# The layout of the split activations in SBUF for 14,928 products of 288 columns: one run of 288 or four blocks of 72

## The chip, the cores and the metric

The kernel runs on one core of a Trainium2 chip. The metric is the time of one execution on the device, in microseconds (us). All inputs, weights and outputs are float32.

## What is computed

One layer of a streaming encoder for 288 tokens (256 of a prompt, 32 of a sample), which share all weights:

```
x = x + 0.5 * (silu(h @ w_gate) * (h @ w_up)) @ w_down      h = rmsnorm(x)      D = 2048, D_FF = 5504
z = rmsnorm(x) @ w_in                                       37 strips of 128 columns
x = x + concat(A, B, C) @ w_out                             A sparse, B windowed, C banded attention
x = x + 0.5 * (silu(h @ w_gate) * (h @ w_up)) @ w_down      second set of weights
```

Keys and values of the three attentions are outputs too. Nearly all arithmetic is in the eight weight matrices; the attention works on 288 tokens only.

## The kernel before, in words

**Products.** Activations lie with the features on the partitions and the 288 tokens along the free dimension. A weight matrix comes from HBM in strips of 128 output features: a strip is up to 16 tiles of 128 by 128 (15 or 14 in the down projections, whose 43 input tiles are taken in thirds). To get more precision out of the one-pass type float32r, each operand is split in an upper and a lower part: `w_hi` is the weight rounded to float32r (ScalarE, line 1056), `w_lo` the rest (VectorE, line 1367), and likewise `h_hi`/`h_lo` for the normalized input, `gu_hi`/`gu_lo` for the gated product, `o_hi`/`o_lo` for the attention's output. For each tile of a strip TensorE makes three products into the same PSUM bank (lines 601 to 603, in `products`): w_hi times hi, w_lo times hi, w_hi times lo. Each has its own weight load. There are 3 x (3344 + 1376 + 256) = 14,928 of them.

**The right sides.** `right_side` (line 144) gives each of the six activation arrays tiles of TILE = 320 float32 columns, of which columns 24 (PAD) to 311 hold the 288 tokens. `products` reads them backwards, `t[:, ::-1]`, and writes the bank backwards too (lines 598 and 600), so the result stands in its normal order.

**Who writes the right sides.** `h_hi` ScalarE line 1066 and `h_lo` VectorE lines 1376 and 1616; `gu_hi` ScalarE line 1273 and `gu_lo` VectorE line 1692; `o_hi` ScalarE line 1136 and `o_lo` VectorE line 1489. Tile 5 of `o_hi` and of `o_lo` (`key_hi`, `key_lo`) serves for a time as room for squares, which POOL writes and TensorE reads forwards at lines 660 and 661. The first two tiles of `gu_hi` serve as data for ten warm-up products (line 912).

**Order.** Each engine runs its own program; semaphores join them. TensorE goes through the strips of a phase (up, down, prep, cb, a, wo) in a loop; before the first tile of each half strip it waits for that half's `w_lo` (`lo_rdy`), before a strip for the bank two strips back to be read (`evac`). ScalarE and VectorE split the following strip while TensorE multiplies this one; SP's queue loads the strip after that. The weight buffers are double. In a "down" phase TensorE waits at tile 0 for all but the last gated tile and at the last tile for the last one (`gu_when`, line 967); in the first strip after a "down" or "wo" phase it waits before each tile k for `h_lo` of that tile (`h_when`, line 941).

**Other products.** The mean of squares for a norm is one product of 288 columns in plain float32 (line 648), which the profile shows as two passes, each with a weight load. The attention's scores, transposes and outputs are smaller products between the strips of cb and a.

Of the kernel before, what the change touches and what calls it, by code (L numbers as in the profile page):

```python
# [7 lines left out]
ALU = mybir.AluOpType  # L8
ACT = mybir.ActivationFunctionType
AX_X = mybir.AxisListType.X  # L10
F32 = mybir.dt.float32


F32R = mybir.dt.float32r

P = 128
# [97 lines left out]
def encoder_step(nc, x, cak, cav, caki, cbk, cbv, cck, ccv, w_in, w_out, qk_norm, sinks, c_bias, t5_bias,  # L114
# [6 lines left out]
    NT = T_P + T_S  # L121
# [9 lines left out]
    ctx = ExitStack()  # L131
    with ctx:
        def sb(name, shape, dt=F32, scope=ctx):
            return scope.enter_context(nc.sbuf_tensor(name, shape, dt))
# [7 lines left out]
        xT = x_room[:, 3 * DT:3 * DT + DT * NT].rearrange("p (k n) -> p k n", n=NT)  # L142
        def right_side(name, tiles, scope=ctx):
            room = sb(name, [P, tiles, TILE], F32R, scope)
            return room[:, :, PAD:PAD + NT], room

        TILE = -(-NT // 64) * 64
        PAD = 24
        h_hi, _ = right_side("h_hi", DT)
        h_lo, _ = right_side("h_lo", DT)  # L150
        raw = [sb(f"raw{s}", [P, 16, P]) for s in range(2)]
# [6 lines left out]
        with ExitStack() as ffn_scope:  # L158
            gu_hi, gu_room = right_side("gu_hi", thirds[0], ffn_scope)
            gu_lo, _ = right_side("gu_lo", thirds[0], ffn_scope)  # L160
        o_hi, _ = right_side("o_hi", 16)
        o_lo, _ = right_side("o_lo", 16)

# [9 lines left out]
        table_first = sb("table_first", [P, 3])  # L173
        warm = gu_room[:, 0:2, :].rearrange("p k n -> p (k n)")[:, 0:512]

# [30 lines left out]
        sq_set = [t[:, 0:NT] for t in sq_wide]  # L206
        key_hi, key_lo = o_hi[:, 5, :], o_lo[:, 5, :]
        sqx = sq
# [383 lines left out]
        def _(pe):  # L592
            def products(ph, j, s, rhs, ks, n, first_k, last_k, when=None, bank=None):

                for k in ks:
                    if when:
                        when(k)
                    hi, lo = (t[:, ::-1] for t in rhs(k))
                    b = buf(ph, s)
                    out = (bank or bank_w[b])[:, 0:NT][:, ::-1]  # L600
                    pe.matmul(out, w_hi[b][:, k, :], hi, start=(k == first_k), stop=False)  # L601
                    pe.matmul(out, w_lo[b][:, k, :], hi, start=False, stop=False)  # L602
                    mm = pe.matmul(out, w_hi[b][:, k, :], lo, start=False, stop=(k == last_k))  # L603
                return mm
# [24 lines left out]
            def h_rhs(k):  # L629
                return h_hi[:, k, :], h_lo[:, k, :]  # L630

            def gu_rhs(k):
                return gu_hi[:, k, :], gu_lo[:, k, :]

            def o_rhs(k):
                return o_hi[:, k, :], o_lo[:, k, :]

# [385 lines left out]
        def _(act):  # L1023
# [41 lines left out]
            def h_upper(index, j):  # L1065
                act.activation(h_hi[:, j, :], xT[:, j, :], ACT.Copy, scale=g_cols[:, bass.ds(j + index * DT, 1)]).then_inc(hhi_rdy, 1)

# [66 lines left out]
            def out_hi(U, p, tile):  # L1134
                act.wait_ge(pv_done, U + (3 * p + 3))
                act.activation(o_hi[:, tile, :], bank_o[:, 0:NT], ACT.Copy).then_inc(ohi_rdy, 1)

# [106 lines left out]
            for ph in phases:  # L1244
                if ph.name == "up":
                    F0 = sum(p.more["size"] for p in phases[:phases.index(ph)] if p.name == "up")

                    def body(j, ph=ph, F0=F0):
# [23 lines left out]
                        act.wait_ge(gu_rdy, F + 1)  # L1272
                        act.activation(gu_hi[:, j, :], gu[:, :], ACT.Copy).then_inc(guh_rdy, 1)  # L1273
                    bodies(act, ph, body, peel_first=3 if ph.n0 == 0 else ph.more["first"])
# [68 lines left out]
        def _(dve):  # L1343
# [26 lines left out]
            def h_tile(index, j):  # L1370
                H = j + DT * index
                dve.wait_ge(sqx_rdy, H + (1 - DT))
                dve.wait_ge(acc_rdy, H)
                dve.tensor_tensor(sumsq[:, :], sumsq[:, :], sqx[:, :], ALU.add).then_inc(acc_rdy, 1)
                dve.wait_ge(hhi_rdy, H + 1)
                dve.scalar_tensor_tensor(h_lo[:, j, :], xT[:, j, :], g_cols[:, bass.ds(j + index * DT, 1)],
                                         h_hi[:, j, :].bitcast(F32), ALU.mult, ALU.subtract).then_inc(hlo_rdy, 1)

# [108 lines left out]
            def out_lo(body, p, tile):  # L1487
                dve.wait_ge(ohi_rdy, body * 2 + (p + 1))
                dve.tensor_tensor(o_lo[:, tile, :], bank_o[:, 0:NT], o_hi[:, tile, :].bitcast(F32), ALU.subtract).then_inc(olo_rdy, 1)

# [119 lines left out]
            def first_piece(i):  # L1610
# [3 lines left out]
                def lower(t):  # L1614
                    dve.wait_ge(hhi_rdy, t + 1)
                    dve.scalar_tensor_tensor(h_lo[:, t, :], xT[:, t, :], g_cols[:, t:t + 1], h_hi[:, t, :].bitcast(F32),
                                             ALU.mult, ALU.subtract).then_inc(hlo_rdy, 1)
# [33 lines left out]
            for ph in phases:  # L1651
                if ph.name == "up":
                    F0 = sum(p.more["size"] for p in phases[:phases.index(ph)] if p.name == "up")

                    def body(j, ph=ph, F0=F0):
# [35 lines left out]
                        dve.wait_ge(guh_rdy, F + 1)  # L1691
                        dve.tensor_tensor(gu_lo[:, j, :], gu[:, :], gu_hi[:, j, :].bitcast(F32), ALU.subtract).then_inc(gul_rdy, 1)  # L1692
                    bodies(dve, ph, body, peel_first=3 if ph.n0 == 0 else ph.more["first"])
# [339 lines left out]
```

## Time and profile before

| | us |
|---|---|
| median of 3 runs | 2054.03 (2053.9 to 2054.44) |
| the profiled execution, its own time | 2054.93 |
| span of the profiled execution, first to last instruction | 2053.4 |
| TensorE busy / VectorE busy / ScalarE busy / POOL busy | 2046.0 / 1170.1 / 846.2 / 88.5 |
| mean rate of the DMA queues | 166 GB/s |

A product's duration in the profile (about 295 ns) is its latency; products overlap, so what counts is the distance between the starts of two neighbours. The times in order of time are in us from the start of the span, to 0.01 us. "PEld" is the weight load of a product.

### The profile page before, as it was taken

Reading aid. Unit: us, or ns where it says so; the run is one execution under the profiler, and the core shown is the slowest. Engines: PE = TensorE matmul, PEld = TensorE weight load, DVE = VectorE, ACT = ScalarE, POOL = GpSimd, SP = SyncE. Lnnn points to the kernel's source line nnn. Section 1 sums busy time; section 2 is a strip of 40 time slices with the busy share of each in tenths; the row PEclk is TensorE's granted clock in tenths of the full one; section 3 lists DMA queues with packets and bytes.
Section 4 is the critical chain, followed back from the end, with each engine's and each line's share of the span. In section 5 each row is a group of like instructions: output and inputs, shape, how many; then the busy total and the mean of one; then the engine's idle time right before and its main releaser. Section 6 shows DMA issues by size and latency. Waiting matters only on the chain.

```text
span 2053.4 us, 41905 instructions
## 1 busy us (share of the span) xinstructions
PE 2046.0 (100%) x15805; PEld 2026.2 (99%) x15805; DVE 1170.1 (57%) x1790; ACT 846.2 (41%) x1290; POOL 88.5 (4%) x140
## 2 busy tenths in 40 slices
PE   9999999999999999999999999999999999999999
PEld 8999999999999999999999999999999999999999
DVE  7555445554455556588889755555445555455544
ACT  6333333333333344345668644333333333333332
POOL 0000000000000000022432000000000000000000
PEclk9999999999999999999999999999999999999999
DMA  7544555545545545544443455555544555545554
GB/s 260 164 163 160 173 163 170 171 162 161 176 158 170 169 156 178 178 143 157 152 153 111 148 164 164 167 170 168 172 160 164 168 166 168 171 163 165 168 183 144
DMA packets 101274, 339.96 MB, mean 166 GB/s; under 512 B 12149, under 2 KB 16293, under 8 KB 101200
## 3 DMA queue, kind: packets, MB, share of 16 engines
q1 hardware_dynamic: 95856, 329.41, 49.0%
q0 software_dynamic: 2960, 7.45, 1.3%
q10 hardware_dynamic: 2400, 2.33, 0.3%
q8 instruction: 36, 0.59, 0.1%
q14 instruction: 22, 0.18, 0.0%
HBM read 334.45 MB, written 5.28 MB: 165 GB/s over the span
## 4 chain that ended last, share of the span: by engine, by line
PE 97%; DVE 1%; ACT 1%; issue 0%; DMA 0%; SPq 0%; DVEq 0%; ACTq 0%
PE bank L601 31%; PE bank L603 31%; PE bank L602 31%; PE bank L688 1%; PE bank L721 1%; PE bank L703 1%; PE bank L665 0%; DMA raw<-in_w_ffn_up 0%; DVE w_lo L1367 0%; PE bank L903 0%; ACT w_hi L1056 0%; ACT s_buf L1113 0%; PE bank L705 0%; DVE z_prep L1448 0%; ACT z_prep L1113 0%
## 5 line engine op out<-in xcount | busy, mean ns | idle before, releaser
L601 PE MATMUL bank<-h_hi,w_hi 128*128 128x288 f32 x3344 | 989.4, 296 | 2.3 <-DVE w_lo L1624 2.0
L603 PE MATMUL bank<-h_lo,w_hi 128*128 128x288 f32 x3344 | 986.3, 295 | 0.0
L602 PE MATMUL bank<-h_hi,w_lo 128*128 128x288 f32 x3344 | 985.1, 295 | 0.0
L1367 DVE TENSOR_TENSOR w_lo<-raw,w_hi 128x1024 fp32r<-128x1024 f32 x634 | 729.7, 1191 | 206.6 <-ACT w_hi L1056 206.2
L1056 ACT ACTIVATE w_hi<-raw 128x1024 fp32r<-128x1024 f32 x634 | 617.0, 1020 | 321.0 <-PE bank L603 318.2
L601 PEld LDWEIGHTS bank<-h_hi,w_hi 128*128 128x128 f32 x3344 | 628.7, 188 | 6.9 <-DVE w_lo L1624 3.2
L602 PEld LDWEIGHTS bank<-h_hi,w_lo 128*128 128x128 f32 x3344 | 628.9, 188 | 0.2
L603 PEld LDWEIGHTS bank<-h_lo,w_hi 128*128 128x128 f32 x3344 | 628.8, 188 | 0.0
L603 PE MATMUL bank<-gu_lo,w_hi 128*128 128x288 f32 x1376 | 405.9, 295 | 0.0
L601 PE MATMUL bank<-gu_hi,w_hi 128*128 128x288 f32 x1376 | 405.2, 294 | 0.0
L602 PE MATMUL bank<-gu_hi,w_lo 128*128 128x288 f32 x1376 | 405.2, 294 | 0.0
L601 PEld LDWEIGHTS bank<-gu_hi,w_hi 128*128 128x128 f32 x1376 | 258.7, 188 | 0.0
L602 PEld LDWEIGHTS bank<-gu_hi,w_lo 128*128 128x128 f32 x1376 | 258.7, 188 | 0.0
L603 PEld LDWEIGHTS bank<-gu_lo,w_hi 128*128 128x128 f32 x1376 | 258.7, 188 | 0.0
L1273 ACT ACTIVATE gu_hi<-gu 128x288 f32 (+1 forms) x86 | 38.2, 445 | 384.0 <-DVE gu L1689 384.0
L1729 DVE SCALAR_TENSOR_TENSOR gains_and_x<-bank,gains_and_x 128x288 f32 (+1 forms) x96 | 43.9, 457 | 192.1 <-PE bank L603 191.1
L1269 ACT ACTIVATE g_sig<-g_act 128x288 f32<-128x288 f32 x86 | 38.2, 444 | 274.0 <-DVE g_act L1391 274.0
L1391 DVE TENSOR_TENSOR u_act<-bank,rstd 128x288 f32<-128x288 f32 x86 | 39.3, 457 | 156.3 <-PE bank L603 156.3
L1391 DVE TENSOR_TENSOR g_act<-bank,rstd 128x288 f32<-128x288 f32 x86 | 39.3, 457 | 108.2 <-PE bank L603 108.0
L1692 DVE TENSOR_TENSOR gu_lo<-gu,gu_hi 128x288 f32 (+1 forms) x86 | 39.4, 459 | 69.1 <-ACT gu_hi L1273 69.1
L601 PE MATMUL bank<-o_hi,w_hi 128*128 128x288 f32 x256 | 76.1, 297 | 0.0
L603 PE MATMUL bank<-o_lo,w_hi 128*128 128x288 f32 x256 | 75.5, 295 | 0.0
(205 smaller groups left out, 985.6 us busy)
## 6 DMA issues: line engine op xcount, KB each, us to landing
raw<-in_w_ffn_gate SPq DMA_DIRECT2D x168, 512.0 KB, 4.5
raw<-in_w_ffn_up SPq DMA_DIRECT2D x168, 512.0 KB, 4.6
raw<-in_w_ffn_down SPq DMA_DIRECT2D x96, 512.0 KB, 3.8
raw<-in_w_in SPq DMA_DIRECT2D x74, 512.0 KB, 4.7
raw<-in_w_ffn_down SPq DMA_DIRECT2D x64, 384.0 KB, 4.2
raw<-in_w_out SPq DMA_DIRECT2D x32, 512.0 KB, 4.5
raw<-in_w_ffn_down SPq DMA_DIRECT2D x32, 448.0 KB, 4.4
bias_rev<-bias_vectors POOLq DMA_DIRECT2D x11, 256.0 KB, 4.6
```

Of the source, the lines that this page charges most:

```text
L601: pe.matmul(out, w_hi[b][:, k, :], hi, start=(k == first_k), stop=False)
L602: pe.matmul(out, w_lo[b][:, k, :], hi, start=False, stop=False)
L603: mm = pe.matmul(out, w_hi[b][:, k, :], lo, start=False, stop=(k == last_k))
L688: mm = pe.matmul(bank_s[c][:, b * T_P:b * T_P + NKEY[r]], q[half, FULL[r]], kt[half, KEY0[r]:KEY0[r] + NKEY[r]], start=True, stop=True)
L703: mm = pe.transpose(bank_t[b][:, o:o + P], s_buf[slot][:, c, kc * P:(kc + 1) * P], ident[:, :])
L1056: act.activation(w_hi[b][:, k, :], raw_tile(ph, j, s)[:, k, :], ACT.Copy).then_inc(hi_rdy, 1)
L1269: act.activation(g_sig[:, :], g_act[:, :], ACT.Silu).then_inc(sig_rdy, 1)
L1273: act.activation(gu_hi[:, j, :], gu[:, :], ACT.Copy).then_inc(guh_rdy, 1)
L1367: dve.tensor_tensor(w_lo[b][:, k, :], raw_tile(ph, j, s)[:, k, :], w_hi[b][:, k, :].bitcast(F32), ALU.subtract)\
L1391: return dve.tensor_tensor(dst, (early_bank(n) or bank_w[b])[rows, cols], rstd[rows, cols], ALU.mult)
L1692: dve.tensor_tensor(gu_lo[:, j, :], gu[:, :], gu_hi[:, j, :].bitcast(F32), ALU.subtract).then_inc(gul_rdy, 1)
L1729: dve.scalar_tensor_tensor(dst, src[:, 0:NT], factor, xT[:, d, :], ALU.mult, ALU.add)\
```

## The change

The upper and the lower array of each pair become one room with 320 columns per tile and some columns over at the end. In a tile, token 72a + b (a from 0 to 3, b from 0 to 71) lies at column 24 + 80a + b; so a tile is four runs of 72 columns with gaps of 8 columns, and the last run of a tile ends in column 335, that is, 16 columns into the next tile's 320. The products read (a, b) with both directions reversed; the bank is written in the same order as before, token 287 first, through a pattern of 4 by 72 whose addresses are adjacent. The instructions that write the right sides (lines 1066, 1376, 1616, 1273, 1692, 1136, 1489) now write, and where they read the upper part back read, four runs of 72; their other operands are seen as 4 by 72 with no gap. Number of instructions, order, semaphores, weights, loads and the number of columns per product do not change. `key_hi`, `key_lo` and the warm-up tile stay one run. The h room grows by 64 columns, so all arrays behind it move by 256 bytes.

The diff, without its unchanged lines:

```
--- before.py
+++ after.py
@@ -140,14 +140,16 @@
-        def right_side(name, tiles, scope=ctx):
-            room = sb(name, [P, tiles, TILE], F32R, scope)
-            return room[:, :, PAD:PAD + NT], room
-        TILE = -(-NT // 64) * 64
-        PAD = 24
-        h_hi, _ = right_side("h_hi", DT)
-        h_lo, _ = right_side("h_lo", DT)
+        def right_sides(name, tiles, scope=ctx, tail=0):
+            room = sb(name, [P, 2 * tiles * TILE + tail], F32R, scope)
+            spread = room[:, PAD:PAD + 2 * tiles * TILE].rearrange("p (t a b) -> p t a b", a=NT // BLOCK, b=APART)[:, :, :, 0:BLOCK]
+            return spread[:, 0:tiles], spread[:, tiles:2 * tiles], room
+        def blocks(row):
+            return row.rearrange("p (a b) -> p a b", b=BLOCK)
+        BLOCK, APART, TILE, PAD = 72, 80, 320, 24
+        h_hi, h_lo, _ = right_sides("h_hi_and_lo", DT, tail=64)
@@ -156,10 +158,8 @@
-            gu_hi, gu_room = right_side("gu_hi", thirds[0], ffn_scope)
-            gu_lo, _ = right_side("gu_lo", thirds[0], ffn_scope)
-        o_hi, _ = right_side("o_hi", 16)
-        o_lo, _ = right_side("o_lo", 16)
+            gu_hi, gu_lo, gu_room = right_sides("gu_hi_and_lo", thirds[0], ffn_scope, tail=PAD)
+        o_hi, o_lo, o_room = right_sides("o_hi_and_lo", 16, tail=PAD)
@@ -171,7 +171,7 @@
-        warm = gu_room[:, 0:2, :].rearrange("p k n -> p (k n)")[:, 0:512]
+        warm = gu_room[:, 0:512]
@@ -204,7 +204,7 @@
-        key_hi, key_lo = o_hi[:, 5, :], o_lo[:, 5, :]
+        key_hi, key_lo = (o_room[:, t * TILE + PAD:t * TILE + PAD + NT] for t in (5, 16 + 5))
@@ -595,9 +595,9 @@
-                    hi, lo = (t[:, ::-1] for t in rhs(k))
+                    hi, lo = (t[:, ::-1, ::-1] for t in rhs(k))
-                    out = (bank or bank_w[b])[:, 0:NT][:, ::-1]
+                    out = blocks((bank or bank_w[b])[:, 0:NT])[:, ::-1, ::-1]
@@ -627,13 +627,13 @@
-                return h_hi[:, k, :], h_lo[:, k, :]
+                return h_hi[:, k, :, :], h_lo[:, k, :, :]
-                return gu_hi[:, k, :], gu_lo[:, k, :]
+                return gu_hi[:, k, :, :], gu_lo[:, k, :, :]
-                return o_hi[:, k, :], o_lo[:, k, :]
+                return o_hi[:, k, :, :], o_lo[:, k, :, :]
@@ -1063,7 +1063,7 @@
-                act.activation(h_hi[:, j, :], xT[:, j, :], ACT.Copy, scale=g_cols[:, bass.ds(j + index * DT, 1)]).then_inc(hhi_rdy, 1)
+                act.activation(h_hi[:, j, :, :], blocks(xT[:, j, :]), ACT.Copy, scale=g_cols[:, bass.ds(j + index * DT, 1)]).then_inc(hhi_rdy, 1)
@@ -1133,7 +1133,7 @@
-                act.activation(o_hi[:, tile, :], bank_o[:, 0:NT], ACT.Copy).then_inc(ohi_rdy, 1)
+                act.activation(o_hi[:, tile, :, :], blocks(bank_o[:, 0:NT]), ACT.Copy).then_inc(ohi_rdy, 1)
@@ -1270,7 +1270,7 @@
-                        act.activation(gu_hi[:, j, :], gu[:, :], ACT.Copy).then_inc(guh_rdy, 1)
+                        act.activation(gu_hi[:, j, :, :], blocks(gu[:, :]), ACT.Copy).then_inc(guh_rdy, 1)
@@ -1373,8 +1373,8 @@
-                dve.scalar_tensor_tensor(h_lo[:, j, :], xT[:, j, :], g_cols[:, bass.ds(j + index * DT, 1)],
-                                         h_hi[:, j, :].bitcast(F32), ALU.mult, ALU.subtract).then_inc(hlo_rdy, 1)
+                dve.scalar_tensor_tensor(h_lo[:, j, :, :], blocks(xT[:, j, :]), g_cols[:, bass.ds(j + index * DT, 1)],
+                                         h_hi[:, j, :, :].bitcast(F32), ALU.mult, ALU.subtract).then_inc(hlo_rdy, 1)
@@ -1486,7 +1486,7 @@
-                dve.tensor_tensor(o_lo[:, tile, :], bank_o[:, 0:NT], o_hi[:, tile, :].bitcast(F32), ALU.subtract).then_inc(olo_rdy, 1)
+                dve.tensor_tensor(o_lo[:, tile, :, :], blocks(bank_o[:, 0:NT]), o_hi[:, tile, :, :].bitcast(F32), ALU.subtract).then_inc(olo_rdy, 1)
@@ -1613,7 +1613,7 @@
-                    dve.scalar_tensor_tensor(h_lo[:, t, :], xT[:, t, :], g_cols[:, t:t + 1], h_hi[:, t, :].bitcast(F32),
+                    dve.scalar_tensor_tensor(h_lo[:, t, :, :], blocks(xT[:, t, :]), g_cols[:, t:t + 1], h_hi[:, t, :, :].bitcast(F32),
@@ -1689,7 +1689,7 @@
-                        dve.tensor_tensor(gu_lo[:, j, :], gu[:, :], gu_hi[:, j, :].bitcast(F32), ALU.subtract).then_inc(gul_rdy, 1)
+                        dve.tensor_tensor(gu_lo[:, j, :, :], blocks(gu[:, :]), gu_hi[:, j, :, :].bitcast(F32), ALU.subtract).then_inc(gul_rdy, 1)
```

## Rows read from the trace of the kernel before

**Rows 1.** The page, its head and parts 1 and 2 (TensorE's granted clock in 40 slices)

```profile
span 2053.4 us, 41905 instructions
...
PE 2046.0 (100%) x15805; PEld 2026.2 (99%) x15805; DVE 1170.1 (57%) x1790; ACT 846.2 (41%) x1290; POOL 88.5 (4%) x140
...
PEclk9999999999999999999999999999999999999999
```

**Rows 2.** The page, part 4: the chain that ended last, shares by engine and line

```profile
PE 97%; DVE 1%; ACT 1%; issue 0%; DMA 0%; SPq 0%; DVEq 0%; ACTq 0%
PE bank L601 31%; PE bank L603 31%; PE bank L602 31%; PE bank L688 1%; PE bank L721 1%; PE bank L703 1%; PE bank L665 0%; DMA raw<-in_w_ffn_up 0%; DVE w_lo L1367 0%; PE bank L903 0%; ACT w_hi L1056 0%; ACT s_buf L1113 0%; PE bank L705 0%; D
```

**Rows 3.** Groups by line, TensorE, line 601: busy us, mean ns of one, idle time before

```profile
L601 PE MATMUL bank<-h_hi,w_hi 128*128 128x288 f32 x3344 | 989.4, 296 | 2.3 <-DVE w_lo L1624 2.0 <-DVE g_act L1391 0.3
...
L601 PE MATMUL bank<-gu_hi,w_hi 128*128 128x288 f32 x1376 | 405.2, 294 | 0.0
...
L601 PE MATMUL bank<-o_hi,w_hi 128*128 128x288 f32 x256 | 76.1, 297 | 0.0
```

**Rows 4.** Busy time by window, two long stretches of the feed-forward blocks

```profile
60.00:760.00 700.00, 700.00 (x5341) 700.00 (x5341) 354.97 (x433) 255.76 (x317) 0.00 (x0) 1.00 0.51 166
...
1240.00:2040.00 800.00, 800.00 (x6102) 799.89 (x6101) 402.90 (x484) 291.44 (x354) 0.00 (x0) 1.00 0.51 168
```

**Rows 5.** TensorE in order of time, 799.81 to 802.17 us: start, duration, instruction

```profile
799.81 0.29 PE L603 MATMUL bank<-gu_lo,w_hi 128*128 128x288 f32 x1
799.94 0.29 PE L601 MATMUL bank<-gu_hi,w_hi 128*128 128x288 f32 x1
...
802.17 0.29 PE L603 MATMUL bank<-gu_lo,w_hi 128*128 128x288 f32 x1
```

**Rows 6.** TensorE in order of time, around the mean of squares at 35.41 us

```profile
35.41 0.65 PE L648 MATMUL bank<-kt_c,mean_d 128*128 128x288 f32 x2
35.68 0.51 PE L601 MATMUL bank<-h_hi,w_hi 128*128 128x288 f32 x1
36.03 0.29 PE L602 MATMUL bank<-h_hi,w_lo 128*128 128x288 f32 x1
```

**Rows 7.** TensorE in order of time, the two forward products at 927.17 us

```profile
927.17 0.29 PE L660 MATMUL bank<-o_hi,mean_hd 128*128 128x288 f32 x1
927.30 0.30 PE L661 MATMUL bank<-o_lo,mean_hd 128*128 128x288 f32 x1
927.44 1.40 PE L665 MATMUL bank<-mean_hd,z_prep 128*128 128x2 f32 x12
```

**Rows 8.** Weight loads in order of time, the twelve narrow products at 927.31 us

```profile
927.31 1.44 PEld L665 LDWEIGHTS bank<-mean_hd,z_prep 128*128 128x128 f32 x12
928.67 0.19 PEld L601 LDWEIGHTS bank<-h_hi,w_hi 128*128 128x128 f32 x1
```

**Rows 9.** Groups by line: five of the seven ScalarE and VectorE lines that the change reshapes

```profile
L1692 DVE TENSOR_TENSOR gu_lo<-gu,gu_hi 128x288 f32 (+1 forms) x86 | 39.4, 459 | 69.1 <-ACT gu_hi L1273 69.1
...
L1273 ACT ACTIVATE gu_hi<-gu 128x288 f32 (+1 forms) x86 | 38.2, 445 | 384.0 <-DVE gu L1689 384.0
...
L1066 ACT ACTIVATE h_hi<-gains_and_x 128x288 fp32r<-128x288 f32 (+1 forms) x48 | 24.4, 522 | 2.5 <-DMA gains_and_x<-in_gains_and_x 2.5
...
L1376 DVE SCALAR_TENSOR_TENSOR h_lo<-gains_and_x,h_hi (+1 forms) x32 | 16.6, 518 | 3.4 <-ACT h_hi L1066 2.2
...
L1489 DVE TENSOR_TENSOR o_lo<-bank,o_hi 128x288 fp32r<-128x288 f32 (+1 forms) x16 | 7.2, 450 | 2.9 <-ACT o_hi L1136 2.9
```

**Rows 10.** Groups by line: ScalarE copies written in two pieces

```profile
L1105 ACT ACTIVATE v_c<-bank 128x256 f32<-128x256 f32 x5 | 1.9, 384 | 15.9 <-PE bank L673 15.9
...
L1105 ACT ACTIVATE v_a<-bank 128x256 f32<-128x256 f32 x2 | 0.8, 384 | 8.8 <-PE bank L673 8.8
```

**Rows 11.** Waits of TensorE: what it waited for, us in total, times, longest

```profile
PE bank L601 <- DVE w_lo L1624: 2.0, 2, 1.2
```

## The prediction

> **What bounds the kernel now.** I read the head of the page first: TensorE is busy for 2046.0 of 2053.4 us, and its granted clock is full (2.4 GHz) in all forty slices [rows 1]. The chain of waits says the same: 97% of it is TensorE, and three lines, 601 to 603, hold 31% each [rows 2]. "Busy" could hide slack, so I looked at the groups by line: the whole group at line 601 has 2.3 us of idle time ahead of it, and the list of waits holds 2.0 us at this line for `w_lo`, in two waits [rows 3, 11]. No buffer and no other engine holds these products up.
>
> So the number that matters is the distance between the starts of two neighbours. In two long stretches 700 us hold 5341 products and 800 us hold 6102: 131.1 ns each [rows 4]. In order of time, 18 steps from 799.81 to 802.17 us are 2.36 us, again 131.1 ns [rows 5]. Line 601 has 3344 + 1376 + 256 = 4976 products [rows 3]; three lines make 14,928, and 14,928 x 131.1 ns = 1957 us. The other 96 us of the span are the start, the attention's products and the end. One ns on the distance is 14.9 us, 0.73% of the time. The bound for "no change" is 0.2%, 4.1 us, about what a measurement of this kernel can tell from nothing; that is 0.28 ns per product, two thirds of one column's time.
>
> **What is in the 131.1 ns.** A column at 2.4 GHz takes 0.417 ns, 288 take 120.0 ns. That leaves 11.1 ns, 166 us of the whole kernel. Three rows say where they can and can't come from. The loads of weights by themselves can follow each other every (928.67 - 927.31) / 12 = 113 ns [rows 8], less than 120, so a load alone doesn't set the distance. The plain float32 product of the norm runs in two passes of 288 columns, also with a load each; from its start at 35.41 us to the start of the second product behind it at 36.03 us are 0.62 us, less one usual step of 0.13 makes 0.245 us per pass [rows 6]: twice the column time (0.240) and some 3 to 5 ns. So with the same number of columns and loads, but half the speed of reading, the excess is 3 to 5 ns, and at full speed it is 11. About 8 ns (11.1 - 3) appear only when the right side is read at one column per clock. Those are what a layout of the right side could touch: 8 x 14.9 = 121 us at most. The two products that read forwards, at 927.17 and 927.30 us, have steps of 0.13 and 0.14 us [rows 7], so even turning the whole direction moves little more than the 0.01 us that these rows resolve.
>
> **The change part by part.**
>
> *The reading of the right side.* It has three breaks per product (four runs of 72, gaps of 8 columns, 32 bytes). No product of before reads with a break, so the cost has to be bounded. Best case: the 8 ns vanish, -121 us. Worst case by a near scale: each break costs one clock of the slower level, 1.2 GHz, 0.83 ns; 3 x 0.83 x 14,928 = +37 us; one column's time each would be +19 us. My value is 0: the number of columns is the same; runs and gaps are multiples of 8 columns, and the starts (24, 104, 184, 264) are too, so no small group of columns that was read whole before is cut now; and the nearest row with broken addresses, ScalarE's copy of 256 elements in two pieces, takes 384 ns both where the pieces adjoin (`v_c`) and where they lie 128 columns apart (`v_a`) [rows 10]. That row is another engine's write, so I keep both ends.
>
> The Trainium skill ("SBUF — State Buffer", the note on cachelines) says that SBUF is read in 16-byte lines, four float32, and that each new line costs. By it nothing changes: 72 lines before, 72 now. No run here has yet shown it. The same note and "PSUM — Partial Sum Buffer" (Specifications) say that a PSUM pattern that isn't contiguous slows products a lot. This speaks against the change if the 4 by 72 pattern of the bank counts as broken; its addresses adjoin, so I take it not to. No row shows which.
>
> *The bank's pattern.* Same order and addresses, written as 4 by 72 instead of 288. Priced like the reading: 0, with the same +19 to +37 us as upper end if each inner wrap costs a clock.
>
> *The seven writing instructions.* Each writes four runs instead of one. Counts are 86 and 86 for `gu`, 48 and 48 for `h`, 16 and 16 for `o`, at 386 to 522 ns each [rows 9]. Even 20% more on all would be 300 x 0.1 = 30 us on two engines that together have over 2000 us idle. Cover: ScalarE waited 384.0 us ahead of `gu_hi` [rows 9]; VectorE is 57% and ScalarE 41% busy [rows 1]; a "down" phase needs the last gated tile only at its last tile, 14 tiles x 3 x 131 ns = 5.5 us after it begins. The `h` tiles after a phase are asked for one by one, one in 0.39 us against about 0.52 us on each of two engines, but most are made while the last strips still run; TensorE's list of waits shows none for them. Without cover are only the first tiles at the start: a few times 0.1 us. I take 0, and +1 us as upper end.
>
> *Weights.* They move by 256 bytes with the h room. The distance is the same for h and gu tiles, in stretches far apart [rows 4, 5], so the place of one array against another seems not to matter: 0.
>
> Sum: 0 in the middle. The profiled execution's own time is 2054.93 us, 1.5 above its span; the median of the runs is 2054.03. On the median the forecast is **2054.0 us**.
>
> **Rivals.**
>
> *Same.* The 8 ns belong to the boundary of two products (the next stream of columns starting at full speed behind a load), not to the addresses. For it: the distance is the same, to 0.1 ns, in all arrays and all stretches, whatever else is running. Against it: the row at half speed shows that the reading matters somehow. Chance 0.42.
>
> *Faster.* The 8 ns are lost in the course of reading one long unbroken run, and the gaps let the read run past the place where it loses. All of it gone gives 2054 - 121 = 1933 us; a quarter, 2 ns, gives 2024, and small steps are likelier than all. The Trainium skill ("TensorE: Matmul & The Clock Gate", Back-to-back issue gap) gives N/2.4 + 2.5 ns for an undisturbed product, so 122.5 ns here; the trace has 131.1 and disagrees, and by the page an estimated 128 us would be there to be won. For it: the 8 ns exist, and nothing in the loads explains them [rows 6, 8]. Against: nothing says that gaps are what helps. Chance 0.30.
>
> *Slower.* The reader fetches in fixed stretches of memory, and a run that ends inside one makes it fetch that stretch again or start anew. Counted from the tile's start, the old run touches 19 stretches of 16 columns, the new ones 5 each, 20; of 32 columns it is 10 against 12. If the 8 ns are paid per stretch, one more of 19 costs 0.43 ns, +6 us; two more of 10 cost 1.6 ns, +24 us, 2078 us. A clock per break gives +19 to +37. It decides as soon as a product gets 0.28 ns longer. Chance 0.28, middle 2078.
>
> That the change doesn't do what it says would look like "same": if the four-by-seventy-two pattern had no gaps at all. The gaps are in the addresses, so I give it nothing of its own.
>
> **How the numbers follow.** Faster 0.30, same 0.42, slower 0.28, straight from the cases. The range must leave out at most 0.2: I cut the large gains (over 50 us, 0.12) and what lies beyond a clock per break at 2091 (0.04). So 2004 to 2091 us, 0.84. The likeliest case's own range is 2050 to 2058.
>
> **What would show it.** Right: products 131.1 ns apart in the windows at 60 to 760 us, groups at 601 to 603 with the same mean of about 295 ns, TensorE's waits still about 2 us, and the writing lines within a few per cent of 386 to 522 ns. Faster: a distance below 130.8 in all stretches alike, h, gu and o, with the other 96 us unchanged. Slower by the reader: a distance longer by the same amount everywhere. Wrong in another way: an unchanged distance but idle time ahead of line 601 with `h_lo` or `gu_lo` behind it.

## The result, and the profile after

The changed kernel takes 2038.15 us (median of 4 runs, 2037.59 to 2038.41), the kernel before, timed beside it, 2053.97. The ratio is 0.9922 [0.9905, 0.9939]: 0.78% faster. The range 2004 to 2091 holds it; the direction does not fit, for the likeliest case was "no change". It is the rival "Faster", with a small step.

Head, busy times and chain of the page of after, beside [rows 1, 2]:

```profile
span 2036.6 us, 41985 instructions
...
PE 2030.4 (100%) x15805; PEld 2010.1 (99%) x15805; DVE 1169.9 (57%) x1790; ACT 846.6 (42%) x1290; POOL 88.5 (4%) x140
...
PE 97%; DVE 1%; ACT 1%; issue 0%; DMA 0%; SPq 0%; DVEq 0%; ACTq 0%
```

Only TensorE's time changed: it is 15.6 us less busy, the span is 16.8 us shorter, and the other engines have the same busy time to 0.4 us. The working instructions are the same in number; the 80 more that the head counts are address arithmetic of VectorE's sequencer. Busy time in the first window of [rows 4] (us, then per engine PE, PEld, DVE, ACT, POOL with counts, granted clock, DMA share, GB/s):

```profile
60.00:760.00 700.00, 700.00 (x5387) 700.00 (x5386) 359.65 (x439) 259.16 (x321) 0.00 (x0) 1.00 0.51 168
```

5387 products instead of 5341: 700 / 5387 = 129.9 ns apart. TensorE in order of time, eighteen steps in a stretch of `gu` products, beside [rows 5]:

```profile
799.72 0.29 PE L603 MATMUL bank<-gu_hi_and_lo,w_hi 128*128 128x288 f32 x1
...
802.06 0.29 PE L603 MATMUL bank<-gu_hi_and_lo,w_hi 128*128 128x288 f32 x1
```

2.34 us / 18 = 130.0 ns. Over many products the distance is 131.11 ns before and 130.00 after, in `h`, `gu` and `o` alike. The difference, 1.11 ns, times 14,928 is 16.6 us; the span lost 16.8, the median 15.8. So the gain lies in the spacing of the products, and other causes add up to about 1 us at most. The groups of the writing lines, beside [rows 9], and TensorE's waits, beside [rows 11]:

```profile
L1692 DVE TENSOR_TENSOR gu_hi_and_lo<-gu,gu_hi_and_lo 128x288 f32 (+1 forms) x86 | 39.4, 459 | 76.5 <-ACT gu_hi_and_lo L1273 76.5
...
L1273 ACT ACTIVATE gu_hi_and_lo<-gu 128x288 f32 (+1 forms) x86 | 38.3, 446 | 379.5 <-DVE gu L1689 379.5
...
L1066 ACT ACTIVATE h_hi_and_lo<-gains_and_x 128x288 fp32r<-128x288 f32 (+1 forms) x48 | 24.4, 522 | 2.7 <-DMA gains_and_x<-in_gains_and_x 2.7
...
L1376 DVE SCALAR_TENSOR_TENSOR h_hi_and_lo<-gains_and_x,h_hi_and_lo (+1 forms) x32 | 16.5, 517 | 3.8 <-ACT h_hi_and_lo L1066 2.4
```

```profile
PE bank L912 <- DVE gu_hi_and_lo L1601: 1.7, 1, 1.7
PE bank L705 <- DVE z_prep L1484: 0.6, 1, 0.6
PE bank L601 <- DVE g_act L1391: 0.4, 1, 0.4
PE bank L601 <- DVE w_lo L1624: 0.4, 2, 0.2
```

Writing four runs instead of one changes none of the seven lines by more than 2 ns per instruction. At line 601 TensorE waits 1.6 us less for `w_lo` than before; the other waits differ by 0.2 us at most.

### The profile page after: what moved, and what is told of

Same layout as the page of the kernel before. It is cut to its first block, busy times and chain, and to the rows that moved or that the text cites. A ratio compares the mean times of both kernels' runs of the same rounds, so it can differ in the third digit from the quotient of the medians.

```text
span 2036.6 us, 41985 instructions
## 1 busy us (share of the span) xinstructions
PE 2030.4 (100%) x15805; PEld 2010.1 (99%) x15805; DVE 1169.9 (57%) x1790; ACT 846.6 (42%) x1290; POOL 88.5 (4%) x140
## 4 chain that ended last, share of the span: by engine, by line
PE 97%; DVE 1%; ACT 1%; issue 0%; DMA 0%; SPq 0%; DVEq 0%; ACTq 0%
PE bank L601 32%; PE bank L603 31%; PE bank L602 31%; PE bank L688 1%; PE bank L721 1%; PE bank L703 1%; PE bank L665 0%; DVE w_lo L1367 0%; PE bank L903 0%; DMA raw<-in_w_ffn_up 0%; ACT w_hi L1056 0%; ACT s_buf L1113 0%; PE bank L705 0%; DVE z_prep L1448 0%; ACT z_prep L1113 0%
## 5 line engine op out<-in xcount | busy, mean ns | idle before, releaser
L601 PE MATMUL bank<-h_hi_and_lo,w_hi 128*128 128x288 f32 x3344 | 985.0, 295 | 0.8 <-DVE g_act L1391 0.4
L602 PE MATMUL bank<-h_hi_and_lo,w_lo 128*128 128x288 f32 x3344 | 980.2, 293 | 0.0
L603 PE MATMUL bank<-h_hi_and_lo,w_hi 128*128 128x288 f32 x3344 | 980.2, 293 | 0.0
L601 PEld LDWEIGHTS bank<-h_hi_and_lo,w_hi 128*128 128x128 f32 x3344 | 629.0, 188 | 6.0 <-issue 2.5
L602 PEld LDWEIGHTS bank<-h_hi_and_lo,w_lo 128*128 128x128 f32 x3344 | 629.2, 188 | 0.2
L603 PEld LDWEIGHTS bank<-h_hi_and_lo,w_hi 128*128 128x128 f32 x3344 | 629.0, 188 | 0.0
L601 PE MATMUL bank<-gu_hi_and_lo,w_hi 128*128 128x288 f32 x1376 | 403.2, 293 | 0.0
L603 PE MATMUL bank<-gu_hi_and_lo,w_hi 128*128 128x288 f32 x1376 | 403.2, 293 | 0.0
L602 PE MATMUL bank<-gu_hi_and_lo,w_lo 128*128 128x288 f32 x1376 | 403.2, 293 | 0.0
L603 PEld LDWEIGHTS bank<-gu_hi_and_lo,w_hi 128*128 128x128 f32 x1376 | 258.7, 188 | 0.0
L601 PEld LDWEIGHTS bank<-gu_hi_and_lo,w_hi 128*128 128x128 f32 x1376 | 258.7, 188 | 0.0
L602 PEld LDWEIGHTS bank<-gu_hi_and_lo,w_lo 128*128 128x128 f32 x1376 | 258.7, 188 | 0.0
L601 PE MATMUL bank<-o_hi_and_lo,w_hi 128*128 128x288 f32 x256 | 75.6, 295 | 0.0
L602 PE MATMUL bank<-o_hi_and_lo,w_lo 128*128 128x288 f32 x256 | 75.0, 293 | 0.0
```

## The experiments

Layouts are named so: the *run* is before's (288 columns in one piece), the *blocks* are after's (4 of 72, 80 apart); the *start* is the column of the tile at which the first piece begins, 24 in both. Seen from the weights (modulo 64 columns) it is 24 too, since tiles and arrays are multiples of 64 columns. "Backwards" is the direction of both kernels.

The theories. **A**: gaps by themselves help, more or other gaps help more. **B**: only the right side's own alignment counts. **C**: the load of the next weights, running beside the product, disturbs its reading; in its first form a shorter load would disturb less, in its second form (**C2**) what counts is where the right side's reads stand relative to the load's reads, in address and in rhythm. **D**: the layout has no part in it. **F**: the right side is read against a fixed rhythm of the engine; its own place counts, and the place of the weights is no part of it.

Five of the ten kernels are *series*: the whole layer is left out, the outputs are not computed, and only long series of products like those of lines 601 to 603 are run, one layout after another, with `w_hi`, `w_lo`, `w_hi` and the tiles of the upper and lower part in turn. Nothing else runs beside them. They were run once each. Their times mean nothing; what is read is the distance of the products.

### Which part of the layout moves the distance

One pair of lines makes each series; for the blocks and for a start at column 16:

```
-  side(which == 2, k, 288)
+  side(which == 2, k, 288, blocks=4, apart=80)
+  side(which == 2, k, 288, pad=16)
```

> This kernel leaves the whole layer out. It only loads a slab of x and one strip of weights, splits nothing, and makes 45 series of 144 products each (three per tile as in the layer: two with one right side, one with the other), every series with another layout of right side, weights or bank. In order of time one series is one row, so the distance of two products is the step between the rows' starts divided by 144. The first two series (one run of 288 read backwards) should give 131.1 ns and the blocks 72/80 backwards 130.0 ns if the products alone explain the result. Theory A, the gaps help the reading: more gaps help more (8 x 36 below 4 x 72 below 2 x 144 below one run), where the run starts in the tile doesn't matter. Theory B, alignment: the distance depends on the start column within a small group of columns; other pads of the single run reach 130.0 or less, and the blocks lose their gain at other pads. Theory C, collision with the weight load that runs beside the product: moving the weights by 4 to 48 columns changes the distance by as much as moving the right side does, and the direction of reading matters. Theory D, a fixed cost at each product's boundary: 128 to 384 columns differ by exactly 0.417 ns per column and no layout matters. bf16 (half the bytes) should fall to about 120 + 3 ns under A, B and C, and stay at 131 under D.

TensorE in order of time: first product of a series of 144, and first of the next one; the run backwards (166), the run forwards (168), the blocks (170), then the blocks at start 16 (194):

```profile
60.08 0.29 PE L166 MATMUL bank<-right,w_hi 128*128 128x288 f32 x1
...
78.95 0.29 PE L168 MATMUL bank<-right,w_hi 128*128 128x288 f32 x1
...
98.15 0.29 PE L170 MATMUL bank<-right,w_hi 128*128 128x288 f32 x1
...
116.88 0.29 PE L172 MATMUL bank<-right,w_hi 128*128 128x288 f32 x1
...
326.62 0.30 PE L194 MATMUL bank<-right,w_hi 128*128 128x288 f32 x1
...
345.82 0.30 PE L196 MATMUL bank<-right,w_hi 128*128 128x288 f32 x1
```

18.87 / 144 = 131.0 ns; 19.20 / 144 = 133.3; 18.73 / 144 = 130.1; 19.20 / 144 = 133.3. The series has both distances of the two kernels without any other engine at work, so D falls and the place of the effect is found: the reading by TensorE. The rest of the table, in ns:

| what | distance |
|---|---|
| run, start 8, 12, 24, 28 | 131.1 |
| run, start 16 or 32 / 0, 4 or 20 | 131.7 / 133.3 |
| the run read as 4 by 72 without gaps | 131.1 |
| blocks, start 0, 8, 16, 32 | 133.3 |
| 4 blocks 76 or 88 apart, 2 of 144, 8 of 36, 3 of 96 | 133.3 |
| 9 pieces of 32, 36 apart | 130.6 |
| run, weights 4 or 8 / 16 or 32 / 48 columns further on | 131.7 / 131.1 / 132.0 |
| run, bank written forwards, or in blocks with gaps | 131.1 |
| run, always the same right tile | 131.1 |
| run or blocks forwards | 133.3 |
| run of bf16, either direction | 122.5 |
| run of 128 / 192 / 256 / 320 / 384 columns, start 0 | 111.3 / 111.9 / 118.5 / 146.7 / 177.8 |

Of the five starts of the blocks only 24 gains; of the other gapped patterns only 9 pieces of 32 do (130.6), the rest are slower than the run. That speaks against A. Read as 4 by 72 without gaps the run keeps its 131.1 ns, so the form of the pattern does nothing, and the addresses decide. The bank's pattern costs nothing. The Trainium skill ("PSUM — Partial Sum Buffer", Specifications) says that a PSUM pattern that isn't contiguous slows products significantly; this series had one with gaps and was as fast as without, so the measurement decides against it here. And what is lost is lost in reading: over the column time (N x 0.417 ns) the excess at start 0 is 11.8 ns for 256 columns, 13.3 for 288 and 320, 17.8 for 384. It grows with the length, so it is no fixed price of a boundary between products.

### The blocks, and the run, read forwards

```
-                    hi, lo = (t[:, ::-1, ::-1] for t in rhs(k))
+                    hi, lo = rhs(k)
-                    out = blocks((bank or bank_w[b])[:, 0:NT])[:, ::-1, ::-1]
+                    out = blocks((bank or bank_w[b])[:, 0:NT])
```

> The changed kernel with right sides and bank read and written forwards. Under C (collision with weight loads, which run in one fixed direction) and whatever else depends on direction, the gain of the blocks needs the backward order: distance above 130.0 ns, 2045 to 2080 us. Under A and B, in which only the addresses of the right side count, it stays within 0.2% of the changed kernel, 2038 us.

Measured 2086.04 us, 1.015 [1.0133, 1.0167] of before. The window of 60 to 760 us:

```profile
60.00:760.00 700.00, 700.00 (x5252) 700.00 (x5251) 347.70 (x421) 249.11 (x306) 0.00 (x0) 1.00 0.50 163
```

700 / 5252 = 133.3 ns. The same gaps that gained 16 us backwards lose 32 us forwards. A and B, which had put 2038 us, miss by 48 us; C's range, up to 2080, was too small by 6 us.

```
-                    hi, lo = (t[:, ::-1] for t in rhs(k))
+                    hi, lo = rhs(k)
-                    out = (bank or bank_w[b])[:, 0:NT][:, ::-1]
+                    out = (bank or bank_w[b])[:, 0:NT]
```

> The kernel before with right sides and bank in forward order (one run of 288). Under A or B no more than 0.5% from the kernel before, 2054 us; under C longer: the two forward products of the kernel before had steps of 0.13 and 0.14 us, so 131.5 to 135 ns, 2060 to 2110 us.

The kernel before with the same edit took 2064.87 us, 1.0046 [1.003, 1.0063]; its window holds 5319 products, 131.6 ns. By itself this doesn't separate the theories, for A and B had allowed up to 0.5%. At start 24 the gain needs both, the gaps and the direction: forwards the blocks are 21 us behind the run, backwards 16 us ahead of it. But the direction too counts only together with the place. A later series has the blocks read forwards at start 16 (254); with the first product of the series behind it:

```profile
847.17 0.29 PE L254 MATMUL bank<-right,w_hi 128*128 128x288 f32 x1
...
865.89 0.29 PE L256 MATMUL bank<-right,w_hi 128*128 128x288 f32 x1
```

18.72 / 144 = 130.0 ns, as backwards at start 24. The first series had 133.3 for the forward run at start 24, a later one and this kernel 131.7: for this layout the distance isn't the same in all surroundings, and why is open.

### The load: fewer columns, other columns, other places

```
-  weight(w[which], k)
+  weight(w[which], k, cols=32)
```

> Like the first series kernel this leaves the whole layer out and makes 78 series of 144 products, each with another layout. The first one spoke for theory C: it gave 131.1 ns for the run and 130.0 for the blocks, but moving the weights changed the run's distance too, direction mattered, and many layouts shared 133.3 ns. [...] Under theory A (gaps help by themselves) or B (alignment of the right side alone) 64 or 32 weight columns leave 131 ns, the shifts of the weights do nothing, and every second column does nothing.

With 128, 96, 64 and 32 weight columns the run's distance is 131.1, 131.1, 131.7 and 133.3: a shorter load made it longer, never shorter. C in its first form falls. (The blocks have 130.0 ns with 32 weight columns and 131.1 with 64, in the next series.) For products of 512 columns it is 233.3 with 128 and with 64 weight columns (213.3 of columns). Loads of every second column, for which the author took C to give less than 126 ns, left the run at 131.1 at all four shifts; with every fourth column the distance is 235. The run was also taken to repeat every 16 columns of start, and doesn't: it has 131.1 at 24, 132.0 at 40 and 133.4 at 56. What speaks for C2: weights moved on by some columns act like a start that is smaller by as many. With the weights moved by 48 the run has 132.0, as at start 40 (that is, 24 - 48, modulo 64); seven of nine moves of the run agree so to 0.1 ns. All four moves of the blocks do, with 134.5 for a move of 32 and for start 56 (in the next series). Most starts that are not multiples of 4 columns cost much more: 136.7 at 2 and 6, 137.7 at 23, 140.0 at 26, but 133.4 at 22; this is the one part of B that holds. Pairs of 4-column pieces (two of them 16 apart, pairs 36 apart) at start 8 gave 126.7, the first distance below 130. The blocks at start 24, however, had 131.1 in this series and 130.0 in the one before, so the next question was whether a series depends on the moment at which it begins.

### Does the moment of the beginning matter?

```
+  for r in range(5):                        # five stretches of 48 products
+      one product of 256, 260 or 264 columns  # shifts the beginning of the next stretch
```

> Leaves the whole layer out; 63 series, each of 5 stretches of 48 products. Ahead of each stretch stands one product of 256 to 320 columns, so that the stretches of a series begin at different moments. The second series kernel spoke against the collision with the weight load (32 weight columns: 133.3 ns, 64: 131.7, 128: 131.1) and gave the blocks 131.1 ns once and 130.0 once with nothing changed but what ran before. New theory F: the reading of the right side is tied to a fixed clockwork of 8 ticks of 1.2 GHz (6.67 ns), in which each 16-byte line of a 64-byte group has its turn; all steady distances so far are multiples of it over a few products (131.11 x 3 = 59 x 6.67, 130.0 x 2 = 39 x 6.67, 133.33 = 20 x 6.67, 126.67 = 19 x 6.67). Under F the steady distance depends on start column modulo 16, direction, gaps, and on the moment at which a stretch begins, so several steady values per layout, all on the grid; weight width, weights' place, one weight tile or one right tile change nothing beyond this set. Under C the weight columns' number and place shift the values of all stretches alike. Under F pairs of lines 64 bytes apart (126.7 ns at pad 8) stay at or near 126.7 in most stretches. bf16 with the 80-apart blocks stays at 122.5.

TensorE in order of time: first product of a stretch of 48 and the odd product behind it; the run, the blocks, the run with 32 weight columns, the blocks with the weights 8 columns further on, the pairs at start 8:

```profile
88.59 0.29 PE L179 MATMUL bank<-right,w_hi 128*128 128x288 f32 x1
...
94.89 0.29 PE L175 MATMUL bank<-right,w_hi 128*128 128x284 f32 x1
...
120.68 0.30 PE L181 MATMUL bank<-right,w_hi 128*128 128x288 f32 x1
...
126.92 0.29 PE L175 MATMUL bank<-right,w_hi 128*128 128x288 f32 x1
...
671.58 0.29 PE L215 MATMUL bank<-right,w_hi 128*32 128x288 f32 x1
...
677.98 0.29 PE L175 MATMUL bank<-right,w_hi 128*128 128x284 f32 x1
...
897.58 0.29 PE L229 MATMUL bank<-right,w_hi 128*128 128x288 f32 x1
...
903.98 0.29 PE L175 MATMUL bank<-right,w_hi 128*128 128x288 f32 x1
...
1411.51 0.29 PE L261 MATMUL bank<-right,w_hi 128*128 128x288 f32 x1
...
1417.59 0.29 PE L175 MATMUL bank<-right,w_hi 128*128 128x280 f32 x1
```

Divided by 48: 131.3, 130.0, 133.3, 133.3, 126.7 ns. The layouts of the two kernels have one value in all five stretches, and so have most series: for them the moment of the beginning doesn't matter. In 11 of 62 series the stretches differ by more than 0.6 ns: the run with the weights 32 columns further on has about 131.1 four times and 133.5 once, the blocks at start 0 have 133.3 and 131.6. Such a layout has more than one distance that it can keep, which may be behind the blocks' 131.1 too; that wasn't shown. The blocks at start 24 are at 130.0 here, at 133.3 at starts 8, 16 and 32, and, at start 24, at 133.2 to 134.5 once the weights stand 4, 8, 16 or 32 columns further on. Nothing of the right side changes in those, so B alone falls.

### Other gaps

```
-  side(which == 2, k, 288, blocks=4, apart=80)
+  side(which == 2, k, 288, blocks=36, apart=36, pad=4)     # and 35 more patterns, four starts each
```

> Leaves the whole layer out; 144 series of 3 x 48 products: right sides in blocks of 4 to 144 columns, 4 to 24 columns of gap, at start columns 0, 4, 8 and 12, all backwards, with one odd product ahead of each stretch. Theory F (clockwork of 6.67 ns): values between 123.3 and 140 ns, on the grid over a few products; most at 133.3 (the stream falls out of step at each gap), a few below 130. Theory A (gaps help by themselves): the mean falls with the number of gaps, from 144-column blocks to 4-column ones. I look for a layout in two dimensions with 127 ns or less at every start, which in the whole kernel would be 2054 - 14,928 x 4.4 ns = 1988 us.

Patterns of 72, 36, 24, 18, 12, 9, 8, 6, 3 or 2 pieces, several distances, starts 0, 4, 8 and 12. The distance doesn't follow the number of gaps: 36 pieces give 126.7 to 128.5 when 36 apart (start 0) and 153 when 24 apart, 18 pieces 24 apart 128.9 at start 4 and 136.7 at start 0, many patterns lie at 133.3. A falls.

### Both moved together, and one alone

```
-  weight(w[which], k), side(which == 2, k, 288)
+  weight(w[which], k, shift=8), side(which == 2, k, 288, pad=24 + 8)
```

> Leaves the whole layer out; 86 series of 3 x 48 products. It tells whether the right side's place counts against a fixed clockwork (F) or only against the weights' place (theory C2: the two read streams of a product, right side and weights of the next product, meet in the same part of memory at a rhythm set by their relative place). Right side and weights are both moved by 4, 8, 16 and 32 columns: under C2 the values stay 131.1 (run), 130.0 (blocks) and 126.7 ns (pairs of lines); under F they change as they do when the right side alone moves (run 131 to 133.3, blocks 131 to 133.3). Moving the weights alone by 4 to 32 columns: under C2 pairs of lines move to about 130 ns at some shifts, as right sides at other starts did. The rest looks for better layouts: 3-dimensional ones with 2 to 4 lines a distance apart; I expect none below 123.3 ns and some at 126.7.

Stretches of 48: run with both moved by 8 (323), blocks with both moved by 8 (325), blocks with the weights moved by 56 alone (341), blocks unmoved (345):

```profile
1468.57 0.29 PE L323 MATMUL bank<-right,w_hi 128*128 128x288 f32 x1
...
1474.87 0.29 PE L175 MATMUL bank<-right,w_hi 128*128 128x284 f32 x1
...
1487.78 0.30 PE L325 MATMUL bank<-right,w_hi 128*128 128x288 f32 x1
...
1494.03 0.30 PE L175 MATMUL bank<-right,w_hi 128*128 128x288 f32 x1
...
1639.72 0.29 PE L341 MATMUL bank<-right,w_hi 128*128 128x288 f32 x1
...
1646.11 0.29 PE L175 MATMUL bank<-right,w_hi 128*128 128x284 f32 x1
...
1678.22 0.30 PE L345 MATMUL bank<-right,w_hi 128*128 128x288 f32 x1
...
1684.46 0.29 PE L175 MATMUL bank<-right,w_hi 128*128 128x280 f32 x1
```

131.3, 130.2, 133.1 and 130.0 ns. At start 32 the blocks had 133.3 as long as the weights stayed; with the weights moved along they have 130 again, and so after 16 and 32 columns too. Weights moved by 64 alone change nothing, by 56 alone they cost 3.1 ns. So it is the difference of the two places, modulo 64 columns (256 bytes), that counts, together with the pattern; F falls, C2 holds. It holds for moves by multiples of 8 columns: both moved by 4 gave 133.3 for the run and 131.1 for the blocks.

### The blocks eight columns earlier, in the whole kernel

```
-        BLOCK, APART, TILE, PAD = 72, 80, 320, 24
+        BLOCK, APART, TILE, PAD = 72, 80, 320, 16
```

> The changed kernel with PAD 16 in place of 24, all else equal: the blocks start 8 columns earlier. By theories C2 and F alike the distance goes to 133.3 ns as in the series kernels, 3.33 ns x 14,928 = 50 us more than the changed kernel: 2088 us, slower than the kernel before. By theory A (gaps help by themselves) it stays at 2038 us.

```profile
60.00:760.00 700.00, 700.00 (x5252) 700.00 (x5251) 348.24 (x422) 248.87 (x306) 0.00 (x0) 1.00 0.50 163
```

2087.23 us, 1.0158 [1.0141, 1.0175]: 133.3 ns in the window. The same gaps, the same number of everything, 32 bytes earlier: 49 us slower than after, 33 us slower than before.

### The weights eight columns earlier, h left in place

```
-        h_hi, h_lo, _ = right_sides("h_hi_and_lo", DT, tail=64)
+        h_hi, h_lo, _ = right_sides("h_hi_and_lo", DT, tail=56)
```

Everything behind the h room moves by 32 bytes: the weights, `gu` and `o`. The `h` tiles don't.

> The changed kernel with 56 instead of 64 spare columns behind the h room: weights, gu and o all lie 8 columns (32 bytes) lower, h stays. So h and weights change their relative place, gu and o keep theirs. C2: the 10,032 products with h go to about 133.3 ns, those with gu and o stay at 130.0: 2038 + 33 = 2071 us. F (a fixed clockwork, the right side's own place): h stays at 130.0, gu and o (4896 products) go to 133.3: 2038 + 16 = 2054 us. A: 2038 us.

2070.16 us, 1.0077 [1.006, 1.0094]. The windows of a "down" phase (`gu` products) and of an "up" phase (`h` products):

```profile
205.00:290.00 85.00, 85.00 (x656) 85.00 (x655) 39.78 (x44) 27.36 (x29) 0.00 (x0) 1.00 0.51 166
300.00:470.00 170.00, 170.00 (x1278) 170.00 (x1277) 85.65 (x105) 62.34 (x80) 0.00 (x0) 1.00 0.49 161
```

85 / 656 = 129.6 ns (130.00 from start to start) where right side and weights moved together, 170 / 1278 = 133.0 (133.33 from start to start) where only the weights moved; windows cut products at both ends. 10,032 `h` products times 3.33 ns are 33.4 us; measured over after are 32.0. One edit that touches no right side of `h` slows exactly the `h` products. This is the clearest run of the study.

### The best pattern of the series, in the whole kernel

```
+                          [[640, tiles], [36, 36], [16, 2], [1, 4]]   # h and gu, upper part from column 8, lower from 40
```

`h` and `gu` are stored as 36 pairs of 4-column pieces, the tiles of upper and lower part woven into each other (so the room stays nearly the same); `o` keeps its blocks. `h_lo` is written in two instructions per tile. To fit, `rinv` takes the room of `sd`, one index buffer that of a mask, and `p_t2` is shortened to the columns that it uses; before it writes `sd`, ScalarE now waits until the key tile that uses `rinv` is normalized.

> The changed kernel with another layout for h and gu: 36 pairs of 4-column lines, the two lines of a pair 16 columns apart, pairs 36 columns apart, tiles woven into each other (tile stride 640 columns, the lower part 32 behind the upper), read backwards; o keeps its blocks. To make room, rinv takes sd's place, idx_acc2 that of a_mask2, and p_t2 is cut to its used columns; h_lo is written by two instructions. Under C2 with the values of the series kernels the 14,160 products with h and gu go from 130.0 to 126.67 ns: 2038.2 - 14,160 x 3.33 ns = 1991 us; the 768 with o stay at 130.0. If the steady state depended on more than relative place and rhythm (weaving of the tiles, loops, the neighbours' products), it would fall back to 130 to 133.3 ns, 2038 to 2087 us. If the writes in bursts of 4 columns are too slow for VectorE or ScalarE, idle time appears ahead of line 601.

1994.67 us, 0.9709 [0.9696, 0.9722] of before, 43 us under after. Window, chain and waits:

```profile
60.00:700.00 640.00, 640.00 (x5055) 640.00 (x5055) 332.96 (x401) 239.91 (x292) 0.00 (x0) 1.00 0.53 172
```

```profile
PE 95%; DVE 3%; ACT 1%; issue 1%; DMA 0%; SPq 0%; DVEq 0%; ACTq 0%
```

```profile
PE bank L615 <- DVE w_lo L1642: 2.0, 4, 0.9
```

640 / 5055 = 126.6 ns. 14,160 products of `h` and `gu` times 3.33 ns are 47.2 us; 43.5 came. The missing 3.7 us are in part longer waits: TensorE waits 2.0 us for `w_lo` instead of 0.4, its listed waits add up to 5.6 us against 3.4 in after, and VectorE has 3% of the chain instead of 1%. That covers 2.2 us; the rest is open.

## Why the prediction was partly right and partly wrong

- **The bound.** Right. The distance of the products sets the time: each ns of it is 14.9 us, and after, forwards, start 16, moved weights and pairs all came out by that rule to within 4 us.
- **Which part can be touched.** Right in kind: of the 11.1 ns of excess some 8 were put down to reading at full speed. The excess grows with the length of the read, bf16 has 2.5 ns of it, and patterns took it from 33 ns (36 pieces 24 apart) down to 6.7 ns (pairs). "It belongs to the boundary of two products", the argument for "Same", is wrong.
- **The reading of the right side: 0.** This is the term of the sum that was missed; it measured -1.11 ns, -16.6 us by the distance and -15.8 by the median. The ends kept for it, -121 and +37 us, hold it. Taking the middle rested on every piece and start being a multiple of 8 columns. That is no protection: start 16 is one as well and costs 49 us against start 24.
- **Weights: "the place of one array against another seems not to matter: 0".** This is the step that failed as reasoning. It was read off a distance equal for `h` and `gu` [rows 4, 5], but all arrays stood at the same place modulo 64 columns, so those rows could not show an influence of the place. The change moves the arrays by exactly 64 columns, so the number 0 came out right by luck; a `tail` of 56 would have made the same change cost 16 us instead of saving 16.
- **The direction.** That turning it "moves little more than the 0.01 us that these rows resolve" [rows 7] is true and tells nothing: 0.01 us on one product is 149 us on all of them. Turned, the run loses 10 us and the blocks lose 48.
- **The rival "Faster".** Right in sign and place, over-sized: it gave 2 ns for "a quarter" and 1.1 came. Its mechanism, gaps that let the read run past the place where it loses, is too simple: of the 144 series with other gaps 12 are faster than the run at start 24, and 123 are slower.
- **The rival "Slower".** Its mechanism, a price per fetched stretch or per break, falls: 36 pairs, 71 breaks, are as fast as any layout that was tried (126.7 ns). But its number, 2078, is near what the same blocks cost at start 16 (2087).
- **Bank pattern, writing instructions, waits.** Right: 0 each, the last two as read from [rows 9, 11].
- **The pages.** By the 16-byte lines of the Trainium skill ("SBUF — State Buffer", the note on cachelines) nothing changes, 72 lines each; the runs show between 126.7 and 153 ns for tiles of 72 whole lines, so the rule doesn't decide here. The Trainium skill's N/2.4 + 2.5 ns ("TensorE: Matmul & The Clock Gate", Back-to-back issue gap), given there for an isolated product, comes out for bf16 with its loads (122.5 measured) and not for float32r.

**What is shown and what isn't.** Shown: TensorE's read of a float32r right side loses time depending on its pattern, its direction and its place relative to the weights that are loaded meanwhile. Not shown is what the two streams meet at inside, and so no rule is had that gives the distance of an untried pattern; the values were found by running them. Also open: why the forward run and, once, the blocks had another distance in another series, and why some layouts change between distances from one stretch to the next.

## What to carry to other kernels

When a kernel is nothing but evenly spaced products, measure their distance over hundreds of steps and compare it with the columns' time; a fraction of a ns is worth microseconds. Equal distances in several arrays say nothing about placement if all of them stand alike: move one array by 32 bytes and look. A series of bare products with one layout after another in a single kernel gives dozens of such prices in one run, and they carried over to the full kernel within 4 us; moving the weights' buffers by a few columns belongs in that series as much as the activations.

## What was not expected of the hardware

- **Two reads of one engine interfere.** `e5` moved only the weights against `h` by 32 bytes: 130.00 became 133.33 ns. The Trainium skill ("SBUF — State Buffer", SBUF: two separate sides, and A bandwidth-pool intuition that's wrong) has TensorE's loads on a second, independent read port, and TensorE waiting on no one. What these runs show is that its products' distance does depend on how the two reads are placed.
- **Of the two types tried only float32r pays.** The same layout in bf16 has 122.5 ns in both directions, and its blocks have the run's distance.
- **Distances fit a grid.** The main steady ones are 131.11, 130.00, 133.33 and 126.67 ns; over three, two, one and one products these are 59, 39, 20 and 19 times 6.67 ns. Single products need not lie on it: the steps of the blocks are 131 and 129 ns in turn, 260 together. What the 6.67 ns are isn't shown.
- **Shorter products reach a floor.** 128, 192 and 224 columns give 111.3, 111.9 and 111.5 ns, near the 113 of [rows 8], where the loads follow each other; that the loads set it is argued from this nearness.
- **The first products are slow.** After 38.8 us without a product the first series began at 0.24 us per product, for some 5 us, though the page gives a full granted clock in every slice:

```profile
39.24 0.44 PE L164 MATMUL bank<-right,w_lo 128*128 128x288 f32 x1
39.48 0.68 PE L164 MATMUL bank<-right,w_hi 128*128 128x288 f32 x2
```

  0.24 us are 288 columns at 1.2 GHz, so here no excess is to be seen, where the prediction read 3 to 5 ns per pass from [rows 6].
